# Gated norms of a two-block transformer kernel: earlier turning, split scaling, and a weight unit's rests on GpSimd

## The reference, cut to what matters

```
n = modulate(rmsnorm_2(h, g_ffn1[l]), sh1, sc1)      # n * (1 + scale) + shift
h = h + 0.5 * gt1 * swiglu(n, w1_gate[l], w1_up[l], w1_down[l])
n = modulate(rmsnorm_2(h, g_mix[l]), sh2, sc2)
h = h + gt2 * hybrid_mixer(n, w_in[l], w_pool[l], pool_scale[l], w_out[l])
n = modulate(rmsnorm_2(h, g_ffn2[l]), sh3, sc3)
h = h + 0.5 * gt3 * swiglu(n, w2_gate[l], w2_up[l], w2_down[l])
```

## Time and profile before

| | |
|---|---|
| time, median of 3 runs | 1086.46 us (1086.25 to 1086.50) |
| profiled execution, first to last instruction | 1084.3 us |
| TensorE busy with products | 1072.6 us, 99% |
| VectorE / ScalarE / GpSimd busy | 73% / 62% / 11% |
| granted TensorE clock, mean | 0.998 of full |

### The profile page before, as it was taken

The page is one execution under the profiler, slowest core; times in us unless marked ns, Lnnn a source line. Parts: engine busy times, 40 slices in busy tenths (PEclk is TensorE's granted clock), DMA queues, the critical chain, the costliest instruction groups (busy, mean ns, idle before and its releaser), DMA issues.

```text
span 1084.3 us, 16107 instructions
## 1 busy us (share of the span) xinstructions
PE 1072.6 (99%) x6102; PEld 915.6 (84%) x6102; DVE 792.8 (73%) x1388; ACT 669.0 (62%) x1182; POOL 120.8 (11%) x212
## 2 busy tenths in 40 slices
PE   9999999999999999999999999999999999999997
PEld 8998888888888998888888788888878978888885
DVE  7767678787876876777676787887885777566575
ACT  7778676565676776766565765454476766445443
POOL 1133110110100531010000000111010210000000
PEclk9999999999999999999999999999999999999999
DMA  9933259888855643687777467878655345565551
GB/s 364 328 115 99 97 198 338 285 301 285 320 196 178 221 146 105 224 303 286 249 271 251 155 230 291 291 254 331 253 174 181 132 155 180 189 194 194 180 188 60
DMA packets 65533, 238.33 MB, mean 220 GB/s; under 512 B 7429, under 2 KB 8613, under 8 KB 64688
## 3 DMA queue, kind: packets, MB, share of 16 engines
q1 hardware_dynamic: 51696, 188.82, 51.3%
q0 software_dynamic: 13040, 47.85, 11.7%
q10 hardware_dynamic: 720, 0.62, 0.2%
HBM read 236.15 MB, written 1.11 MB: 219 GB/s over the span
## 4 chain that ended last, share of the span: by engine, by line
PE 90%; DVE 6%; ACT 2%; issue 1%; DMA 0%; POOL 0%; DVEq 0%; ACTq 0%
PE bank L1694 23%; PE bank L1663 15%; PE bank L1665 14%; PE bank L1664 14%; PE bank L1695 12%; PE bank L1815 2%; DVE w_lo L1136 2%; PE bank L1879 1%; PE bank L1861 1%; PE bank L1853 1%; PE bank L1852 1%; DVE tok L1156 1%; PE bank L1712 1%; PE bank L1761 1%; PE bank L1713 1%
## 5 line engine op out<-in xcount | busy, mean ns | idle before, releaser
L1136 DVE TENSOR_TENSOR w_lo<-raw,w_hi 128x1024 fp32r<-128x1024 f32 x348 | 413.8, 1228 | 71.5 <-ACT w_hi L729 68.5
L729 ACT ACTIVATE w_hi<-raw 128x1024 fp32r<-128x1024 f32 x345 | 348.5, 1051 | 68.0 <-DMA raw<-in_stream 67.7
L1694 PE MATMUL bank<-a_two,w_hi 128*128 128x512 f32 x1088 | 386.6, 399 | 0.0
L1695 PE MATMUL bank<-a_two,w_lo 128*128 128x256 f32 x1088 | 305.3, 281 | 0.0
L1694 PEld LDWEIGHTS bank<-a_two,w_hi 128*128 128x128 f32 x1088 | 204.4, 188 | 49.8
L1695 PEld LDWEIGHTS bank<-a_two,w_lo 128*128 128x128 f32 x1088 | 205.4, 189 | 1.7
L941 ACT ACTIVATE cross<-bank 128x256 f32<-128x256 f32 x136 | 51.3, 381 | 192.1 <-PE bank L1695 192.0
L1663 PE MATMUL bank<-w_lo,hid_hi 128*128 128x512 f32 x432 | 169.5, 392 | 0.1
L1664 PE MATMUL bank<-w_hi,hid_lo 128*128 128x512 f32 x432 | 168.5, 390 | 0.0
L1665 PE MATMUL bank<-w_hi,hid_hi 128*128 128x512 f32 x432 | 168.4, 390 | 0.0
L1385 DVE TENSOR_TENSOR hid_act<-bank,cross 128x256 f32<-128x256 f32 x96 | 39.5, 421 | 89.2 <-ACT cross L941 89.2
(11 more groups left out here) (235 smaller groups left out, 1354.6 us busy)
## 6 DMA issues: line engine op xcount, KB each, us to landing
raw<-in_stream SPq DMA_DIRECT2D x348, 512.0 KB, 4.9
ada_raw<-in_ada POOLq DMA_DIRECT2D x72, 512.0 KB, 5.4
cmpw<-in_stream SPq DMA_DIRECT2D x4, 1024.0 KB, 9.3
rel_band<-rel_scratch POOLq DMA_DIRECT2D x2, 1024.0 KB, 9.7
cum_row<-cum_scratch POOLq DMA_DIRECT2D x4, 512.0 KB, 4.3
gate_row<-gate_scratch POOLq DMA_DIRECT2D x3, 512.0 KB, 6.3
h<-in_x SPq DMA_DIRECT2D x2, 512.0 KB, 4.3
silu_row<-in_c_row POOLq DMA_DIRECT2D x2, 512.0 KB, 6.4
```

The lines of the kernel that those rows point to most:

```text
L729: nc.scalar.activation(w_hi[:, u % RING, part_], raw[:, u % RING, part_], ACT.Copy).then_inc(hi_ready, 1)
L1136: nc.vector.tensor_tensor(w_lo[:, u % RING, part_], raw[:, u % RING, part_], w_hi[:, u % RING, part_].bitcast(F32), ALU.subtract).then_inc ...
L1694: nc.tensor.matmul(ps[bank][:, 0:2 * T], wh[:, k, cols_], a_two[:, :, k, :], start=k == 0, stop=False)
L1695: ins = nc.tensor.matmul(ps[bank][:, T:2 * T], wl[:, k, cols_], a_hi[:, k, :], start=False, stop=k == KT - 1)
```

## The change

1. **Turning of tile 0.** In all three passages it now stands between the third and the fourth of the last six row products (`parts(1, 6, 8)`, `turn_rows`, `parts(1, 7, 8)`).
2. **Turning of tile 1.** In all three passages it now stands between the terms h, r and the term l of tile 0's last group.
3. **Scaling.** VectorE scales columns 512 to 1023 of tile 0, too. ScalarE keeps two pieces of 256.
4. **Weights.** GpSimd makes both rests (`w_lo`) of the unit whose second half it rounds (`second_unit`). VectorE's two `rest_half` calls in each passage are gone. ScalarE rounds that unit's first half before the squares (`gmix`, `gf2`) or right behind tile 0's squares (`gf1`), where it used to stand behind the root.
5. **Rows' split.** A counter of ScalarE's shifts lets it go on without waiting for itself. In `gf1` ScalarE shifts chunk 3 of tile 0, too. `norm_turn`, used in the other passages, is unchanged in effect.
6. **First hidden rows of the gated stages.** ScalarE and VectorE do three weight halves between the tiles and one behind the second, in place of four between them.

```diff
                 return [("dve", 512), ("dve", D)]
-            if t == 1 and name != "last":
+            if (t == 1 or name in SHIFTS) and name != "last":
                 return [("act", 256), ("act", 512), ("dve", D)]
             return [("act", 256), ("act", 512), ("act", D)]
...
-            def round_half(name):
-
-                u = POOL_ROUNDS[name]
+            def second_unit(name):
+
+                u = POOL_UNITS[name]
                 wait_raw(pool, u, 1)
                 pool.wait_ge(hi_ready, 2 * u + 1)
                 pool.tensor_copy(w_hi[:, u % RING, HALF:UNIT], raw[:, u % RING, HALF:UNIT]).then_inc(hi_ready, 1)
+                for part in range(2):
+                    part_ = slice(HALF * part, HALF * part + HALF)
+                    pool.wait_ge(hi_ready, 2 * u + part + 1)
+                    pool.wait_ge(lo_ready, 2 * u + part)
+                    pool.tensor_tensor(w_lo[:, u % RING, part_], raw[:, u % RING, part_], w_hi[:, u % RING, part_].bitcast(F32),
+                                       ALU.subtract).then_inc(lo_ready, 1)
...
@@ -680,7 +697,7 @@
             modulation_weights(ADA_OF["mlp1"][0], ADA_OF["mlp1"][1] + ADA_BUFS)
 
             store_gate(0)
-            round_half("gf1")
+            second_unit("gf1")
             pool.wait_ge(bank_turned, TURN["gf1"] + 8)
             pool.wait_ge(unit_used, FIRST["glu0"] + 3)
...
             def gated_turn(name, gain, shift):
 
+                round_half()
+                left_to_pool(name)
+                squares(name, 0)
+                scale(name, 0)
+                shifted_turn(name, 0, gain, shift, (0,))
+                square_half(name, 1, 0)
+                shifted_turn(name, 0, gain, shift, (1, 2))
+                square_half(name, 1, 1)
+                root(name, 1)
+                shifted_turn(name, 0, gain, shift, (3,))
+                scale(name, 1)
+                shifted_turn(name, 1, gain, shift)
+
+            def fused_turn(name, gain, shift):
+
+                nc.scalar.activation(stat[:, 10, :], stat[:, 9, :], ACT.Sqrt)
+                square_half(name, 0, 0)
+                square_half(name, 0, 1)
+                round_half()
+                left_to_pool(name)
+                root(name, 0)
+                scale(name, 0)
+                shifted_turn(name, 0, gain, shift, (0,))
+                square_half(name, 1, 0)
+                shifted_turn(name, 0, gain, shift, (1,))
+                shift_chunk(name, 0, 2, gain, shift)
+                square_half(name, 1, 1)
+                high_chunk(name, 0, 2)
+                shift_chunk(name, 0, 3, gain, shift)
+                root(name, 1)
+                high_chunk(name, 0, 3)
+                scale(name, 1)
+                shifted_turn(name, 1, gain, shift)
...
                                          ACT.Silu if gated else ACT.Relu).then_inc(row_act, 1)
-                    if t == 0:
-                        for half in range(4):
-                            round_half()
+                    for half in range(((3, 1) if gated else (4, 0))[t]):
+                        round_half()
                 for n, bank in enumerate(HIDDEN_BANKS[name]):
...
+                    if part == 0 and u - 1 in POOL_UNITS.values():
+                        dve.wait_ge(lo_ready, 2 * u)
                     part_ = slice(HALF * part, HALF * part + HALF)
                     nc.vector.tensor_tensor(w_lo[:, u % RING, part_], raw[:, u % RING, part_], w_hi[:, u % RING, part_].bitcast(F32),
                                             ALU.subtract).then_inc(lo_ready, 1)
                     halves[0] += 1
+
+            def left_to_pool(name):
+
+                assert halves[0] == 2 * POOL_UNITS[name]
+                halves[0] += 2
...
+            def rest_chunk(name, t, c):
+
+                dve.wait_ge(act_high, split_no(name, t, c))
+                if not shift_by_act(name, t, c):
+                    dve.wait_ge(rows_shifted, shift_no(name, t, c))
+                ts = slice(t * P, (t + 1) * P)
+                nc.vector.tensor_tensor(a_lo[:, 2 * c:2 * c + 2, ts], shifted[:, c, :, :],
+                                        a_hi[:, 2 * c:2 * c + 2, ts].bitcast(F32), ALU.subtract).then_inc(act_split, 1)
+
+            def second_rows(name, gain, shift):
+
+                shift_chunk(name, 1, 1, gain, shift)
+                rest_chunk(name, 1, 0)
+                shift_chunk(name, 1, 3, gain, shift)
+                for c in (1, 2, 3):
+                    rest_chunk(name, 1, c)
 
...
                 for k in range(2):
                     add(name, sums, gate, 0, k)
                 inverse_root(name, 0)
-                rest_half()
+                scale(name, 0)
+                left_to_pool(name)
                 add(name, sums, gate, 1, 0)
                 shift_chunk(name, 0, 1, gain, shift)
-                turned(name, 0, gain, shift, (0,), False)
+                rest_chunk(name, 0, 0)
                 add(name, sums, gate, 1, 1)
-                turned(name, 0, gain, shift, (1,), False)
+                rest_chunk(name, 0, 1)
+                first_mean(name, 1)
                 shift_chunk(name, 0, 3, gain, shift)
-                first_mean(name, 1)
-                turned(name, 0, gain, shift, (2,))
+                rest_chunk(name, 0, 2)
                 inverse_root(name, 1, True)
                 scale(name, 1)
-                turned(name, 0, gain, shift, (3,))
-                rest_half()
-                turned(name, 1, gain, shift)
+                rest_chunk(name, 0, 3)
+                second_rows(name, gain, shift)
...
                 two_means(0)
                 weigh(0, 1)
                 both_norms_root(0)
-                rest_half()
+                scale(name, 0)
+                left_to_pool(name)
                 add(name, sums, None, 1, 0)
...
-                    nc.tensor.matmul(dst, a_hi[:, 4 * j + k, ts], wl[:, k, :], start=False, stop=False)
+                if "h" in terms:
+                    wait_weights(u + j, half)
+                    pe.wait_ge(act_high, TURN[name] + 4 * t + 2 * j + half + 1)
+                    for k in (2 * half, 2 * half + 1):
...
                 else:
                     parts(0, 3)
                     parts(1, 2)
-                if name not in ("gf1", "last"):
+                if name in SHIFTS:
+                    parts(1, 6, 8)
+                    turn_rows(name, 0)
+                    parts(1, 7, 8)
+                    return
+                if name != "last":
                     turn_rows(name, 0)
                 parts(1, 3)
-                if name == "gf1":
-                    turn_rows(name, 0)
...
                 opening(name, phase, 0, 0, 0)
                 opening(name, phase, 0, 0, 1)
                 opening(name, phase, 1, 0, 0)
-                turn_rows(name, 1)
-                opening(name, phase, 1, 0, 1)
+                if name in SHIFTS:
+                    opening(name, phase, 1, 0, 1, "hr")
+                    turn_rows(name, 1)
+                    opening(name, phase, 1, 0, 1, "l")
+                else:
+                    turn_rows(name, 1)
+                    opening(name, phase, 1, 0, 1)
```

More of the change, by code:

```diff
@@ L475, in build @@
         NORMS = ["mix0", "mlp0", "mix1", "mlp1", "gf1", "gmix", "gf2", "last"]
+        SHIFTS = ("gf1", "gmix", "gf2")
         NORM = {n: 2 * i for i, n in enumerate(NORMS)}
@@ L513, in build, with shift_by_act, shift_no @@
         EPS_FINAL = 1e-5
-        SHIFTS = {"gf1": 0, "gmix": 4, "gf2": 8}
+        def shift_by_act(name, t, c):
+            return c % 2 == 0 or (name, t, c) == ("gf1", 0, 3)
+        def shift_no(name, t, c):
+            all_ = [(n, k, i) for n in SHIFTS for k in range(TT) for i in range(4)]
+            return sum(shift_by_act(*at) == shift_by_act(name, t, c) for at in all_[:all_.index((name, t, c)) + 1])
         SUMS = {n: 3 * i for i, n in enumerate(["out_even", "mlp0", "out_fox", "mlp1", "glu0", "out_dil", "glu1"])}
@@ L763, in root, with turned @@
                     nc.scalar.activation(fin[:, t, 10:11], fin[:, t, 3:4], ACT.Sqrt, bias=fin[:, t, 4:5]).then_inc(root_ready, 1)
-            def turned(name, t, gain, shift=None, chunks=(0, 1, 2, 3)):
+            def turned(name, t, gain, chunks=(0, 1, 2, 3)):
                 m = TURN[name] + 4 * t
@@ new lines, in turned, with shift_chunk @@
+                    ins.then_inc(act_high, 1)
+            def shift_chunk(name, t, c, gain, shift):
+                m = TURN[name] + 4 * t
+                act.wait_ge(bank_turned, m + c + 1)
+                if t == 1:
+                    act.wait_ge(act_split, m - 4 + c + 1)
+                for k in range(2):
+                    kt = 2 * c + k
+                    bank, c0 = turned_at(name, t, c)
+                    if (name, t, kt) != ("gf1", 0, 1):
+                        ins = nc.scalar.activation(shifted[:, c, k, :], ps[bank][:, c0 + k * P:c0 + (k + 1) * P], ACT.Identity,
```

(8 more changed lines are left out.)

129 lines of the change are left out of this document (48 added, 81 removed).

## The result

The change makes the kernel slower: 1091.74 us (median of 5 executions, 1088.23 to 1094.38) against 1086.35 (1086.25 to 1086.50) for the kernel before on the same chip, a ratio of 1.0045 in the record, with the interval 1.0035 to 1.0056 (the two medians alone give 1.0050). The forecast was 1086.4 and its range ended at 1088.4. Beside the median the spread has changed: 0.25 us before, 6 us now. The profiled execution of the changed kernel took 1090.25 us, its span is 1088.1.

A forecast was written before the change was run, and what follows sets the result against it. TensorE, busy for 1072.6 of 1084.3 us, bounds the kernel, so only its waits can be won. Gains of 4.4 us against GpSimd's cost of 4.35 leave nothing: from 1086.46 to 1086.4 us, range 1082.6 to 1088.4.

The forecast's parts named there:

- What is won: TensorE's waits removed in gf1, gmix and gf2, plus the hidden rows' gain, less 0.1: 4.4 us won.
- The new order of the first hidden rows: Gated stages gf1 and gf2: three halves in place of four bring VectorE's product forward, winning 0.7 us in sum.
- the wait for tile 1's first chunk: Each passage, behind tile 1's turning: only two products cover ScalarE's first chunk, a new wait of 0.1 to 0.15 us.
- What GpSimd costs: GpSimd's cast and rests exclude VectorE's two-operand SBUF operations in gmix, gf1 and gf2: 4.35 us lost in sum.
- rival A: Small operations on 128x1 numbers are not held by GpSimd; exclusion costs 1.8 us, time 1083.9; chance 0.2.
- Rival C: GpSimd keeps the way from cast to first rest whenever VectorE waits; cost 6.9 us, time 1089.0; chance 0.1.
- priced at 1.7 us of hold: Each rest on GpSimd excludes VectorE operations with two SBUF operands for 1.7 us, from a wait in `mlp1`.
- rival D: Forecast's order, but a rest on GpSimd excludes for all of 2.39 us; 1.7 more in sum, 1088.1; chance 0.1.
- `gmix`, priced at 0.75: Root 0.33 late, inside 0.35 spare; second rest holds tile 1's L1157 by 1.0, so TensorE waits 0.45 and 0.3.
- `gf1`, priced at 1.6: Cast and first rest make tile 0's root 2.0 us late, with 0.4 spare: 1.6 us lost.
- `gf2`, priced at 2.0: First rest makes an addition 1.65 us late, second holds the next by 1.0; of 2.65, 0.65 are spare.
- the 0.57 and 0.24: TensorE's waits at turning the first hidden rows, 0.57 us in gf1 and 0.24 in gf2, forecast to go.

The follow-up runs named there:

- zeros for the rests: The changed kernel with GpSimd's six subtractions replaced by memsets of zeros, the casts kept: 1083.19 us, ratio 0.997.
- the best one: Changed kernel without GpSimd's subtractions: VectorE makes both rests in its gaps, in gf1 the first between tile 0's additions; weights' rests used behind tile 1's turning: 1081.88 us.
- the filled kernel: The changed kernel with 16 transposes of the identity ahead of each turning of tile 0: 1089.95 us, ratio 1.0033; run again, 1090.33 us.
- GpSimd's rests alone: The kernel before with only this part of the change: GpSimd makes both rests behind its cast: 1093.17 us, ratio 1.0062.
- the subtractions behind the scaling: The changed kernel with GpSimd's six subtractions waiting until tile 0 is scaled: 1092.38 us, ratio 1.0054.
- second rest by GpSimd: The kernel of 1081.88 us (VectorE's rests in gaps, gf1 early) with the second half's rest made by GpSimd: 1088.80 us, ratio 1.0026.
- the repetition: The changed kernel itself, run again on the chip that also ran the version with filled waits: 1091.79 us, ratio 1.0049.

## Why the prediction was wrong, step by step

The forecast was no change and the medians moved by 5.4 us. Three things make that up, by the table and the runs above: the holds cost 5.6 in place of 4.35, about 3.4 were won in place of 4.4, and two falls of the clock, of 1.6 us each, stood in no term (the second of them is inferred, see below). The largest part is the last.

**What is won.** Forecast 4.4. The sum has a slip: the parts that it names for `gf1` (0.4, 0.4 and 0.7, less 0.1 to 0.15) give 1.4 and not 1.6, so 4.2 was its own result. The change's own order wins 3.2 (zeros for the rests). The new order of the first hidden rows was worked out at 0.7 and gave 1.2 alone. The passages gave, without that order's 0.57 and 0.21, 1.3, 0.4 and 0.9 by the table, against 1.4, 1.05 and 1.15. Of this, the wait for tile 1's first chunk was estimated at 0.1 to 0.15 and is 0.30 by the row at 622.91; in `gmix` the cast held an addition by 0.57, where I had taken 0.13. A kernel faster by 4.4 us exists (the best one), but it has another order and other gains, so that its figure is the forecast's is chance.

**What GpSimd costs, sum 4.35: the first step that failed.** The mechanism was right: two operands from SBUF on VectorE against GpSimd's reads, whole instructions, first come first served, and operations on 128x1 numbers are held like large ones (2.17 and 2.20 in place of 0.22), so rival A is out. Rival C (GpSimd keeping the way) is not needed: in `gmix` the addition of 796.98 ran as soon as the cast was over, ahead of the waiting subtraction. The sizes were off:
- A subtraction was priced at 1.7 us of hold. It lasts 2.37 and 2.39 with nobody ahead, and held VectorE for 1.95 (2.17 less 0.22) to 2.2 (2.89 less 0.69) where VectorE asked within some 0.2 us of its start, and for what was left of it where VectorE asked later. I had taken the 1.7 from four rests beside a multiplication whose row was 2.39; rival D, which took the whole row, was nearer. It gave only 1088.1, because it had the same places and no clock. (The sign named for D, a rest of over 2.5 us, did not come; it was set above D's own 2.39.)
- `gmix`, priced at 0.75. I let the cast wait for the addition and put the first subtraction beside nothing but 0.2 of the root. The cast came 0.08 us before the addition, so it and both subtractions fell on tile 0's additions and root: 2.9 us late, 0.35 spare. The table gives 3.7 against the run with zeros, 2.1 without the fall of the clock.
- `gf1`, priced at 1.6: 2.0 (25.00 less 23.03). `gf2`, priced at 2.0: 1.5 (24.67 less 23.13). In `gf1` the held operation is the one that was named (2.30 where near 1.6 was said). In `gf2` it is not: the first subtraction was to go ahead of tile 0's first addition and went behind it, by 0.07 us. It held the second addition instead (2.17), and the second subtraction held the root (0.83 in place of 0.22). That the sum came near there is partly luck.

**The second step that failed, a term put at nothing: the clock.** No term, rival or bound had it, and no reason was given for leaving it out. In the profiled execution one fall costs 1.6 us. With it, 3.4 won (what the run with zeros gains in the three passages), less 2.0, 2.1 and 1.5 of holds, less 1.6, makes 3.8 us slower, the difference of the spans. That this adds up proves little, as the terms are differences out of one table. What stands by itself is the 1.6: it comes from `gf1` with and without a fall, and in `gmix` the filled kernel, without a fall, took 1.5 less. The median lies a further 1.6 above the difference of the spans, which fits one fall more (two are in the second profile of this kernel), but the median execution itself was not profiled. Without falls the kernel would take some 1088.6 us (1086.35 and 3.8, less 1.6), 2.2 more than forecast and just past the range's end; the one execution at a mean clock of 0.999 took 1088.23. The trace of before had it to show: in its last 9 us TensorE is busy for 2.0 and the granted clock is 0.72 in the mean, whereas I had written of waits over 1 us at two places and asked nothing of what comes after them.

```profile
1075.00:1084.00 9.00, 2.00 (x9) 1.31 (x7) 5.74 (x14) 3.56 (x9) 0.00 (x0) 0.72 0.35 117
```

**What would show it.** Right: the waits for the weight rests and the 0.57 and 0.24 are gone, GpSimd shows a cast and two subtractions, the turnings of tile 0 wait over 1 us in `gf1` and `gf2`. Wrong: in `gmix` the addition of tile 1 was not held (0.69), those of tile 0 were, and the turning waited 2.42 us where its delay was to fit into the spare time.

**The exclusion and the subtraction's price.** In `gf1` of the changed kernel a root operation of 0.16 us took 2.30 beside a subtraction. The Trainium skill (SBUF — State Buffer, Who interferes with whom) says that the one that issues first has the shared pair for the whole instruction. The rows of these runs agree, down to requests 0.05 us apart (884.43 and 884.48); only those of the earlier trace rows, 0.02 us apart, stand in the other order. A free subtraction lasts 2.37 to 2.39 us here. The Trainium skill (GPSIMD Engine Reference, Performance versus the Vector engine) leads by its cycles per element to an estimate of 2.2. The trace is a little above, and nearer to that price than to the 1.7.

## What to carry to other kernels

Work moved to GpSimd is not free where VectorE has a chain of small two-operand steps: count every VectorE operation that may ask while the instruction lasts, at the whole of its time, and try both orders where requests lie a tenth apart. VectorE made the second rest itself in 1.22 us behind tile 1's scaling; handed to GpSimd for 2.4 us beside tile 0's root, it cost 6.9 us over three places, a fall of the clock in one of them included. And where TensorE bounds the kernel, a wait of about 2 us can cost 1.6 us more behind it, and makes the time of the kernel vary.

## What the runs showed of the hardware beyond that

- TensorE's granted clock fell to half for 3.4 us behind some waits and not behind others. At the same place of the same kernel the wait was 1.79 us with a fall and 1.80 without. Over the three passages of all profiles the waits with a fall behind them were 1.62 us (`gmix` with GpSimd's rests alone) to 2.45 us long (`gmix` with the subtractions behind the scaling), and one of 2.19 had none, so length alone does not decide. What else does is open. The first row has a fall behind it (`gf1`, second rest by GpSimd), the second has none (`gf2`, GpSimd's rests alone). With the waits filled with transposes of the identity, neither profile had a fall.

```profile
614.56 1.27 PE L1824 MATMUL bank<-par,tok 128*128 128x128 f32 x8 [2.20 <-ACT tok L836]
...
897.91 0.73 PE L1722 MATMUL bank<-w_hi,a_two 128*128 128x512 f32 x2 [2.19 <-DVE a_two L1259]
```

- VectorE's scaling, a multiplication of one 128x512 tile by a number per partition, was held by a subtraction, too: 2.54 us in `gf2` of the repetition, against 0.49 with nobody ahead. It reads only one large operand from SBUF, so counting two-operand steps alone misses it.

```profile
891.76 2.54 DVE L1228 TENSOR_SCALAR tok<-h,stat 128x512 f32<-128x512 f32 x1
```

- Not every pairing holds: gate products and additions that read a bank ran in 0.68 or 0.69 us beside GpSimd in the passages.
